# Last rows of a decoder step: the 32 sample rows laid out as four column quarters on 128 partitions

## What is computed

```
def rms_norm(x, g):
    xf = x.astype(jnp.float32)
    y = xf * lax.rsqrt(jnp.mean(xf * xf, axis=-1, keepdims=True) + EPS)
    return (y * g.astype(jnp.float32)).astype(x.dtype)

    yp = yp + hier_moe(rms_norm(yp, norm2[l]), *moe_w)
    ys = ys + hier_moe(rms_norm(ys, norm2[l]), *moe_w)
yp = rms_norm(yp, norm_f)
ys = rms_norm(ys, norm_f)
```

## Time and profile before

| what | us |
|---|---|
| median of 3 runs | 614.73 |
| lowest and highest run | 613.83, 614.82 |
| the profiled execution, its own time | 613.61 |
| its span, first to last instruction | 612.0 |
| TensorE busy | 587.9 (96%) |
| VectorE busy | 322.5 (53%) |
| ScalarE busy | 234.5 (38%) |
| GpSimd busy | 52.6 (9%) |

### The profile page before, as it was taken

One profiled execution on the slowest core, in us unless ns is written; L12 is line 12 of the kernel. 1 busy time (PEld: TensorE's weight loads), 2 busy tenths in 40 slices (PEclk: granted clock), 3 DMA queues, 4 the chain that ended last, 5 costly groups with the idle time before them and its releaser, 6 DMA issues.

```text
span 612.0 us, 9005 instructions
## 1 busy us (share of the span) xinstructions
PE 587.9 (96%) x2880; PEld 350.1 (57%) x2880; DVE 322.5 (53%) x725; ACT 234.5 (38%) x415; POOL 52.6 (9%) x126
## 2 busy tenths in 40 slices
PE   7999999999999999999999989999999998999985
PEld 4876796867777686777656744343333333333331
DVE  4648788867767686767735873531141111121137
ACT  6451417275664737475535340211111211112224
POOL 1200001000000000000000002131112121121100
PEclk9999999999999999999999999999999999999999
DMA  8431308922223133221299989999999999999995
GB/s 315 137 137 71 138 34 323 408 104 69 77 77 103 43 103 109 71 77 69 79 331 391 384 348 322 364 419 419 419 418 421 419 421 419 421 420 417 415 370 222
DMA packets 34412, 157.65 MB, mean 258 GB/s; under 512 B 6480, under 2 KB 6864, under 8 KB 22992
## 3 DMA queue, kind: packets, MB, share of 16 engines
q1 hardware_dynamic: 28768, 146.51, 61.0%
q0 software_dynamic: 5472, 10.63, 4.7%
q10 hardware_dynamic: 144, 0.15, 0.1%
HBM read 151.87 MB, written 14.17 MB: 271 GB/s over the span
## 4 chain that ended last, share of the span: by engine, by line
PE 76%; DMA 10%; DVE 6%; ACT 3%; SPq 2%; issue 2%; DVEq 0%; ACTq 0%; POOLq 0%
PE ps L2099 14%; PE ps L1680 14%; PE ps L1682 13%; PE ps L1681 13%; PE ps L2128 8%; DMA wslot<-in_wmoe 5%; PE ps L1821 2%; PE ps L1856 2%; DMA raw<-in_wmix 2%; DMA gy<-ytok 1%; SPq L574 1%; PE ps L1803 1%; DMA ytok<-yo,idx 1%; PE ps L1847 1%; DVE wl L1031 1%
## 5 line engine op out<-in xcount | busy, mean ns | idle before, releaser
L2099 PE MATMUL ps<-wslot,xgT 128*64 128x512 f32 x520 | 116.7, 593 | 2.3 <-DMA wslot<-in_wmoe 1.9
L1680 PE MATMUL ps<-xh,wh 128*128 128x512 f32 x256 | 102.5, 400 | 0.0
L1682 PE MATMUL ps<-xl,wh 128*128 128x512 f32 x256 | 99.9, 390 | 0.0
L1681 PE MATMUL ps<-xh,wl 128*128 128x512 f32 x256 | 99.9, 390 | 0.0
L770 ACT ACTIVATE wh<-raw 128x1024 fp32r<-128x1024 f32 x48 | 50.7, 1059 | 120.5 <-PE ps L1682 101.1
L2099 PEld LDWEIGHTS ps<-wslot,xgT 128*64 128x64 f32 x520 | 37.8, 137 | 74.5 <-issue 73.7
L1031 DVE TENSOR_TENSOR wl<-raw,wh 128x1024 fp32r<-128x1024 f32 x48 | 58.6, 1222 | 23.8 <-ACT wh L770 22.5
L2128 PE MATMUL ps<-wslot,hT 128*64 128x512 f32 x272 | 62.2, 599 | 2.6 <-ACT hT L981 1.5
L1580 DVE SCALAR_TENSOR_TENSOR hm<-ps,rt,hs 128x128 f32<-128x128 f32 x24 | 7.3, 347 | 105.0 <-ACT hs L978 105.0
L1680 PEld LDWEIGHTS ps<-xh,wh 128*128 128x128 f32 x256 | 48.1, 188 | 16.1 <-issue 6.7
L1682 PEld LDWEIGHTS ps<-xl,wh 128*128 128x128 f32 x256 | 48.0, 188 | 10.6
(11 more groups left out here) (379 smaller groups left out, 837.4 us busy)
## 6 DMA issues: line engine op xcount, KB each, us to landing
wslot<-in_wmoe SPq DMA_DIRECT2D x87, 1024.0 KB, 18.4
raw<-in_wmix SPq DMA_DIRECT2D x56, 512.0 KB, 4.0
wslot<-in_wmoe SPq DMA_DIRECT2D x8, 512.0 KB, 20.2
gy<-ytok SPq DMA_DIRECT2D x8, 512.0 KB, 8.6
xt<-in_x SPq DMA_DIRECT2D x4, 512.0 KB, 7.8
at<-in_wmoe SPq DMA_DIRECT2D x2, 1024.0 KB, 18.9
x<-in_x SPq DMA_DIRECT2D x4, 512.0 KB, 4.4
xnd<-x SPq DMA_DIRECT2D x4, 512.0 KB, 9.6
```

The source lines that it names most:

```text
L1680: pe.matmul(out, sh, mh_, start=start, stop=False)
L1681: pe.matmul(out, sl, mh_, start=False, stop=False)
L1682: return pe.matmul(out, sh, ml_, start=False, stop=stop)
L2099: l = pe.matmul(ps[CAP * s:CAP * s + CAP, 2, :], xgT[:, c, CAP * s:CAP * s + CAP], first_at[s * 4 + c] if first_at and c < 4 else at0[:, c ...
```

## The change

The sample tile keeps its sums, but on another shape. Column quarter q (columns 256q to 256q+255) of the 32 sample rows goes to partitions 32q to 32q+31, so that 32 x 1024 becomes 128 x 256 in one PSUM bank. For this:

- PE computes each term of the sample tile as four products of 256 columns, each on its own group of 32 columns of the array (`tile_position=(0, 32q)`), where there were two of 512 columns.
- ACT squares 128 x 256. The row sums of the quarters are then 128 numbers; four products with `fold` add them up over the quarters and place the total on all four groups (second bank). ACT takes the root of that from PSUM.
- DVE scales 128 x 256 by it and by a second copy of the norm's weights, `nfq`, whose group q holds quarter q. Four more DMAs fill `nfq` (32 KB each).
- The sample rows of `y` leave in four DMAs of 32 rows x 1 KB instead of one of 32 rows x 4 KB.

```diff
+    nfq = at("nfq", 134 * K, [P, D // 4])
...
             e.dma_start(nf[:], rows[2:3, :].broadcast_to([P, D])).then_inc(const_in, 16)
+            for q in range(4):
+                e.dma_start(nfq[q * S:q * S + S, :], rows[2:3, q * (D // 4):(q + 1) * (D // 4)].broadcast_to([S, D // 4])).then_inc(const_in, 16)
...
                 e.wait_ge(fin_ready, n + 1)
-                e.dma_start(y_tiles[t], yf[0:rowsof(t), t, :]).then_inc(done_out, 16)
+                if t < NT:
+                    e.dma_start(y_tiles[t], yf[:, t, :]).then_inc(done_out, 16)
+            for q in range(4):
+                e.dma_start(y[SEQ:TA, q * (D // 4):(q + 1) * (D // 4)], yf[q * S:q * S + S, NT, 0:D // 4]).then_inc(done_out, 16)
...
+            def squared(n, t, rows_):
+                a.wait_ge(n2_sq, 2 * TILES + n)
+                a.activation(junk3[:, 0:rows_.shape[1]], rows_, ACT.Square, accum_out=ss[:, t:t + 1]).then_inc(n2_sq, 1)
+            def rooted(t, total):
+                a.activation(rstd[:, t:t + 1], total, ACT.Sqrt, scale=1.0 / D, bias=eps[:]).then_inc(fin_sq, 1)
...
+            a.wait_ge(sample_mm, 1)
+            squared(NT, NT, ps[:, SAMPLE_BANK, 0:D // 4])
+            a.wait_ge(sample_mm, 2)
+            rooted(NT, ps[:, SAMPLE_BANK + 1, 0:1])
...
-            d.wait_ge(const_in, NCONST)
+            d.wait_ge(const_in, NCONST + 64)
...
-            final(NT, ps[0:S, SAMPLE_BANK:SAMPLE_BANK + 2, :].rearrange("p b c -> p (b c)"))
+            final(NT, ps[:, SAMPLE_BANK, 0:D // 4], nfq)
...
             def sample_terms(stationary, rows_, start, stop):
-                for h in range(2):
-                    l = pe.matmul(ps[0:S, SAMPLE_BANK + h, :], stationary, rows_[:, h * 512:h * 512 + 512], start=start, stop=stop)
+                for q in range(4):
+                    c = slice(q * (D // 4), (q + 1) * (D // 4))
+                    l = pe.matmul(ps[q * S:q * S + S, SAMPLE_BANK, 0:D // 4], stationary, rows_[:, c], start=start, stop=stop,
+                                  tile_position=(0, S * q), skip_group_check=True)
...
             sample_terms(stk[:], gy[0:3 * S, 0, NT, :], False, True).then_inc(sample_mm, 1)
+            pe.wait_ge(n2_sq, 2 * TILES + NT + 1)
+            for q in range(4):
+                l = pe.matmul(ps[q * S:q * S + S, SAMPLE_BANK + 1, 0:1], fold[:], ss[:, NT:NT + 1], start=True, stop=True,
+                              tile_position=(0, S * q), skip_group_check=True)
+            l.then_inc(sample_mm, 1)
```

More of the change, by code:

```diff
@@ L650, in _ @@
                 e.wait_ge(fin_ready, n + 1)
-                e.dma_start(y_tiles[t], yf[0:rowsof(t), t, :]).then_inc(done_out, 16)
+                if t < NT:
+                    e.dma_start(y_tiles[t], yf[:, t, :]).then_inc(done_out, 16)
+            for q in range(4):
+                e.dma_start(y[SEQ:TA, q * (D // 4):(q + 1) * (D // 4)], yf[q * S:q * S + S, NT, 0:D // 4]).then_inc(done_out, 16)
             e.wait_ge(v_stored, 32)
-            e.wait_ge(done_out, 16 * (TILES + 1))
+            e.wait_ge(done_out, 16 * (TILES + 4))
         @block.gpsimd
@@ L1004, in _ @@
             a.dma_start(st, so[:]).then_inc(done_out, 16)
[L1005 to L1010, removed]
+            def squared(n, t, rows_):
[3 more added lines that the diff above has]
+                a.activation(rstd[:, t:t + 1], total, ACT.Sqrt, scale=1.0 / D, bias=eps[:]).then_inc(fin_sq, 1)
+            for n, t in enumerate(LENGTHS[:NT]):
+                if t == PE_TILE:
                     a.wait_ge(tile_mm, 1)
-                    rows_ = ps[:, PE_BANK:PE_BANK + 2, :].rearrange("p b c -> p (b c)")
+                    squared(n, t, ps[:, PE_BANK:PE_BANK + 2, :].rearrange("p b c -> p (b c)"))
                 else:
                     a.wait_ge(added[t], 1)
-                    rows_ = x1[:, t, :]
-                a.wait_ge(n2_sq, 2 * TILES + n)
-                a.activation(junk3[0:r, :], rows_, ACT.Square, accum_out=ss[0:r, t:t + 1]).then_inc(n2_sq, 1)
+                    squared(n, t, x1[:, t, :])
                 a.wait_ge(n2_sq, 2 * TILES + n + 1)
-                a.activation(rstd[0:r, t:t + 1], ss[0:r, t:t + 1], ACT.Sqrt, scale=1.0 / D, bias=eps[0:r, :]).then_inc(fin_sq, 1)
+                rooted(t, ss[:, t:t + 1])
+            a.wait_ge(sample_mm, 1)
+            squared(NT, NT, ps[:, SAMPLE_BANK, 0:D // 4])
+            a.wait_ge(sample_mm, 2)
+            rooted(NT, ps[:, SAMPLE_BANK + 1, 0:1])
         @block.vector
@@ L1644, in add_last, with final @@
                 d.tensor_tensor(x1[:, t, :], last_sums(t), x1[:, t, :], ALU.add).then_inc(added[t], 1)
-            def final(t, rows_):
-                r = rowsof(t)
+            def final(t, rows_, scales):
                 d.wait_ge(fin_sq, LENGTHS.index(t) + 1)
-                own.then(d.reciprocal(rstd[0:r, t:t + 1], rstd[0:r, t:t + 1]))
-                d.scalar_tensor_tensor(out=yf[0:r, t, :], in0=rows_, scalar=rstd[0:r, t:t + 1], in1=nf[0:r, :],
+                own.then(d.reciprocal(rstd[:, t:t + 1], rstd[:, t:t + 1]))
+                d.scalar_tensor_tensor(out=yf[:, t, 0:rows_.shape[1]], in0=rows_, scalar=rstd[:, t:t + 1], in1=scales[:],
                                        op0=ALU.mult, op1=ALU.mult).then_inc(fin_ready, 1)
-            d.wait_ge(const_in, NCONST)
+            d.wait_ge(const_in, NCONST + 64)
             combine(1)
@@ L1659, in _ @@
             add_last(1, 2)
-            final(0, x1[:, 0, :])
+            final(0, x1[:, 0, :], nf)
             combine(2)
             add_last(2, 3)
-            final(1, x1[:, 1, :])
-            final(2, x1[:, 2, :])
-            final(PE_TILE, ps[:, PE_BANK:PE_BANK + 2, :].rearrange("p b c -> p (b c)"))
-            final(NT, ps[0:S, SAMPLE_BANK:SAMPLE_BANK + 2, :].rearrange("p b c -> p (b c)"))
+            final(1, x1[:, 1, :], nf)
+            final(2, x1[:, 2, :], nf)
+            final(PE_TILE, ps[:, PE_BANK:PE_BANK + 2, :].rearrange("p b c -> p (b c)"), nf)
+            final(NT, ps[:, SAMPLE_BANK, 0:D // 4], nfq)
         @block.tensor
```

## The result

| | before | changed |
|---|---|---|
| median of 22 runs, us | 614.79 | 616.36 |
| lowest and highest, us | 613.83, 616.57 | 614.85, 618.81 |
| profiled execution, own time | 613.61 | 615.29 |
| its span | 612.0 | 613.6 |

The ratio is 1.0025, with a 95% interval of 1.0017 to 1.0033, or 1.0 to 2.0 us. The ratio is not the quotient of the two medians, so it can differ from theirs by some tenths.) That is inside the forecast range (614.1 to 617.1), but on the far side of the 0.2% line that I had given the larger chance of not being crossed.

What follows compares the result with a forecast made beforehand. Bound by the `gy` reads at DMA rate up to DVE's sum at 595.46, then by DVE. End +0.2, root 0, `nfq` +0.6: +0.8 on 614.73, so 615.5 us, range 614.1 to 617.1.

Steps and rivals of the forecast that it cites:

- the 0.2% line: Smallest change a measurement can tell, about 1.23 us; chances given: within 0.67, slower 0.27, faster 0.06.
- DVE's last scaling, 0.48 for 1.27: Scaling of the sample tile at the program's end, 256 columns for 1024: a gain of 0.79 us, on the path.
- Square, `fold`, root without cost: ACT and PE before the last scaling: no cost, root ready at 607.55, covered by tile 3's scaling with 0.33 to spare.
- the dear `fold` row: Profile row of 64 PE instructions, one per 0.12 us with full weight loads; by it the root would lose 0.5 us.
- The end of the program, +0.2: Last scaling and SP's four writes: -0.79 on DVE, +1.33 for the fourth issue, -0.3 for shorter landing, entered as +0.2 us.
- The transfers of `nfq`, +0.6: SP's queue ahead of the `gy` reads: 128 KB more delay every read and DVE's run after it, +0.6 us, bounds 0 and 1.5.
- The lower of the two prices: Delay of the reads by `nfq`, priced as 128 KB at 337 GB/s: 0.39 us.
- The higher price: Delay by `nfq`, priced by the 128 KB of `gy<-x` to 32 partitions, which landed 0.77 us after `nf`.
- The rival by number or narrowness: `nfq`'s four narrow DMAs delay the reads by more than they carry: up to 3.1 us, 618.0 in all; chance 0.20.
- The sentence on the ports that reach 32 partitions: Trainium skill: partitions 0 to 31 reach only 8 of 16 ports, so `nfq`'s 128 KB take about 0.6 us.
- Absorbed: Rival: idle DMA engines at 585 to 587 take `nfq` free, only +0.2 stays, 614.9 us; chance 0.21.
- The signs that were named: Right if `gy` reads reach DVE 0.6 later, last scaling takes 0.48 without a wait, fourth write is issued 1.3 after the first.

Runs made afterwards that it cites:

- Twelve narrow transfers: Kernel before plus twelve unused DMAs of 32 rows x 1 KB, all from one row, in `nfq`'s place in the queue: 618.57 against 615.27 us, ratio 1.0068.
- three wide ones: Kernel before plus three unused DMAs of 128 rows x 1 KB, all from one row, in `nfq`'s place in the queue: 618.40 us, ratio 1.0053.
- the second trace: The kernel before, run again unchanged for another trace on the same chip: ratio 0.9998 to its own kernel.
- one long: Kernel before plus one unused DMA of 96 rows x 4 KB, all from one row, in `nfq`'s place: 616.99 us, ratio 1.0034.

## Why the prediction was right, point by point

- **In all**: the forecast was +0.8 us, the measured difference 1.5 (1.0 to 2.0). It lies within the range because the range was 3 us wide and had `nfq` at up to 1.5 in it. The sign of the change and the place of the loss were right by reasoning. The single best number was half of what came, and one of the two mechanisms behind it was wrong, as said below. By traces, `nfq` at 1.3 (mean of three) and the end at 0.1 to 0.3 make up the whole.
- **DVE's last scaling, 0.48 for 1.27**: the duration is right, measured 0.48. The two rows that it was worked out from (128 and 1024 columns) gave the value to 0.01. But "on the path" was wrong. Behind the scaling stood tile 3's write, and the first packet of the sample rows starts 2.21 us after that write's issue before and 2.18 with the change, though the sample rows were issued 0.78 sooner. The forecast had a gain of 0.79 and let the four issues eat it; the packets show no gain to eat.
- **Square, `fold`, root without cost**: right. The Square took 0.36 (0.38 forecast), the eight small products 0.29 (0.4), the root was ready 0.48 before DVE wanted it (0.33). The narrow row was the right one to take; the dear `fold` row with its full weight loads was not like this case.
- **The end of the program, +0.2**: right in sum, and that is in part luck. The fourth write was issued 1.5 us after the first (1.33 forecast). The part from the last scaling to the end came to 4.03 to 4.09 in four traces with the quarters in four writes. Against 3.95 and 3.92 in the two traces of the kernel before that is +0.1; against all nine traces with an unchanged end (3.68 to 3.95, mean 3.78) it is +0.3. But the sum was made of a gain of 0.79, a loss of 1.33 and a shorter landing of 0.3. The packets show another sum: nothing gained, and 0.3 lost because the sample rows take 1.16 us from first to last packet where they took 0.83. With two queues the issues came sooner and the end did not.
- **The transfers of `nfq`, +0.6**: this is the term that was too small. Measured from the issue of `nf` to the sum of tile 0 it is +0.9, +1.2 and +1.8 in three traces (against the mean of the two traces before, 24.17), and 1.0 (0.2 to 1.9) by timing. The place was right: first in SP's queue, ahead of the reads, with every later step moved by as much. The lower of the two prices, 0.39, is nearly what `nfq`'s own packets take (0.44). What the forecast left out is that its neighbours' 4 KB packets take longer at the same time, by 0.5 to 1.1 us in all. The higher price, 0.77 between the landings of `nf` and `gy<-x`, came nearer, but for another load.
- **The rival by number or narrowness**: it came to its deciding point, 1.03 us, but not by its mechanism. Twelve narrow transfers cost what three wide ones did. The sentence on the ports that reach 32 partitions does not explain the price of `nfq`. It may well bear on the other narrow loads: with `nf` moved away, the window from 600 to 602, in which the copy and the sample rows' reads pass (32 partitions each, different rows, 4 KB packets), has a DMA share of 1.05 at 258 GB/s. No run separates that.
- **Absorbed**: wrong. The idle share at 586 to 587 was of no use; in the changed kernel the share there is 1.03, and the reads still come later.
- **The signs that were named**: counted from DVE's last work for the last pass (585.17, in the second trace 585.68, with the change 585.25), the sum of tile 0 comes 0.8 to 1.4 us later, not 0.6. DVE did not wait before its last scaling, as forecast.
- **The 0.2% line**: I gave 0.67 to "within 0.2%". The measured interval, 0.17 to 0.33%, lies mostly beyond it.

## What to carry to other kernels

When a small operation is reshaped to fill the partitions, count what its new operands need: here a second copy of a 4 KB row cost about as much as the whole operation had taken (0.9 to 1.8 us against 1.27), since its load stood in a first-in first-out queue ahead of reads that the critical path waited for. A load that is needed late belongs behind the ones that are needed first, even when its issue has 9 us to spare; moving `nf` and two small copies that way, without the change, gave 1.3 us. To price such a load, count also what it does to the packets beside it: a mean rate of the window does not tell. Before a saving at the end of a program is entered as a gain, look what the queue behind it is still working off. And measure effects of 1 us by an interval within the trace, between two events near the change, because whole times scatter by more.

## What the runs showed of the hardware that I had not expected

- Loads that copy one DRAM row to many partitions run the engines at a full share but at 226 to 232 GB/s (4 KB packets) and 236 to 260 GB/s (1 KB packets), each with `nf`, where loads of different rows behind the same `nf` reach 317 to 324, and plain reads 404 to 416 in windows of 2 us.
- They slow other packets too: with 384 KB more of one row, the 4 KB packets in the stretch took 1.43 us (twelve narrow) and 2.76 us (one long) more of the 16 engines' time, with 384 KB of different rows 0.08. The trace with three wide ones does not follow: there their own 1 KB packets took 108 ns on average, and the others nothing more.
- The DMA engines do not go in step: the first packet of `nfq` started 4.5 us before weights that were issued ahead of it were there. PE waited up to 2.40 us for them; that the loads behind caused it is likely, not shown.
- A small write issued 0.59 us after one of 512 KB had its first packet only when the large one's packets ran out, 2.15 to 2.18 us after the large one's issue (2.33 on another queue), where a write with nothing ahead has it 0.83 to 0.86 after its own.
- Two queues that issue two small writes each end no sooner than one queue that issues all four: 4.08 us against 4.04 from the last scaling to the end.
- A DMA whose DRAM view starts with a dimension of 4 ran at a DMA share of 0.17 to 0.25 and made the end 1.5 us longer.
